# A two-layer encoder step without the products of constants in TensorE's waits

## What is computed

```python
def trunk_layer(x, pos, p, hist):
    mix, state = token_mixers(rmsnorm(x, p["g_mix_norm"]), pos, p, hist)
    x = x + mix
    return x + hier_moe(rmsnorm(x, p["g_ffn_norm"]), p), state
```

## Time and profile before

| | us |
|---|---|
| median of 3 runs (lowest to highest) | 1468.4 (1466.06 to 1472.69) |
| the profiled execution's own time | 1468.3 |
| its span, first to last instruction | 1466.5 |
| TensorE busy with matmuls | 1375.7 (94%) |
| VectorE, ScalarE, GpSimd busy | 796.3, 637.7, 91.0 |
| mean granted TensorE clock | 0.978 of 2.4 GHz |

### The profile page before, as it was taken

The page is one execution under the profiler, slowest core; times in us unless marked ns, Lnnn a source line. Parts: engine busy times, 40 slices in busy tenths (PEclk is TensorE's granted clock), DMA queues, the critical chain, the costliest instruction groups (busy, mean ns, idle before and its releaser), DMA issues.

```text
span 1466.5 us, 20830 instructions
## 1 busy us (share of the span) xinstructions
PE 1375.7 (94%) x8354; PEld 1120.0 (76%) x8354; DVE 796.3 (54%) x1156; ACT 637.7 (43%) x931; POOL 91.0 (6%) x84
## 2 busy tenths in 40 slices
PE   5998999999999989999889999999999999899996
PEld 5994666799999756776579847569999987567763
DVE  4426535633335357887663284454333443678876
ACT  4327644522324244566442385554222332455551
POOL 0300000000000011100203000000000000111002
PEclk9999899999999999999999999999999999999998
DMA  8224300033115456998912203001233153599965
GB/s 273 73 77 135 115 1 1 1 115 113 60 61 207 176 227 263 410 411 326 289 64 73 68 8 108 1 1 43 73 114 114 58 215 144 209 362 408 420 224 197
DMA packets 95447, 228.78 MB, mean 156 GB/s; under 512 B 14395, under 2 KB 64597, under 8 KB 82389
## 3 DMA queue, kind: packets, MB, share of 16 engines
q1 hardware_dynamic: 83284, 179.93, 33.8%
q0 software_dynamic: 7424, 30.94, 5.8%
q10 hardware_dynamic: 4656, 16.78, 2.8%
HBM read 199.08 MB, written 33.79 MB: 159 GB/s over the span
## 4 chain that ended last, share of the span: by engine, by line
PE 85%; ACT 5%; DVE 5%; DMA 3%; issue 2%; SPq 0%; ACTq 0%; DVEq 0%; POOLq 0%
PE ps L848 10%; PE ps L850 10%; PE ps L849 10%; PE ps L1321 8%; PE ps L1297 4%; PE ps L1299 4%; PE ps L1298 4%; PE ps L874 3%; PE ps L877 2%; PE ps L880 2%; PE ps L1142 2%; DMA rows_back<-xrow_d,row_of 2%; PE ps L1284 2%; PE ps L1199 2%; PE ps L1200 2%
## 5 line engine op out<-in xcount | busy, mean ns | idle before, releaser
L1856 DVE TENSOR_TENSOR work<-work,ps 128x544 f32<-128x544 f32 x48 | 34.6, 721 | 208.9 <-ACT work L1678 208.9
L1678 ACT ACTIVATE work<-ps 128x544 f32<-128x544 f32 x48 | 30.0, 626 | 244.9 <-PE ps L850 244.9
L849 PE MATMUL ps<-xn_r,ksv_r 128*128 128x272 f32 x384 | 110.8, 288 | 0.0
L849 PE MATMUL ps<-xn_r,work_r 128*128 128x272 f32 x384 | 110.7, 288 | 0.0
L766 POOL DMA_INDIRECT rows_back<-xrow_d,row_of x32 | 38.2, 1194 | 1107.9 <-DVE row_of L2231 891.5
L1299 PE MATMUL ps<-ew_r,rows_tok_r 128*128 128x512 f32 x256 | 100.2, 391 | 0.0
L1856 DVE TENSOR_TENSOR ew_r<-ew,gu_hi_a_r 128x2048 fp32r<-128x2048 f32 x32 | 73.1, 2290 | 15.4 <-ACT gu_hi_a_r L1701 15.4
L849 PEld LDWEIGHTS ps<-xn_r,ksv_r 128*128 128x128 f32 x384 | 72.2, 188 | 0.0
L849 PEld LDWEIGHTS ps<-xn_r,work_r 128*128 128x128 f32 x384 | 72.2, 188 | 0.0
L1701 ACT ACTIVATE gu_hi_a_r<-ew 128x2048 fp32r<-128x2048 f32 x32 | 60.7, 1910 | 5.6 <-ACT yo_b L1746 5.6
L1321 PE MATMUL ps<-ew,acts 128*128 128x512 f32 x128 | 59.4, 608 | 1.5 <-DVE acts L2348 1.5
(11 more groups left out here) (397 smaller groups left out, 3895.5 us busy)
## 6 DMA issues: line engine op xcount, KB each, us to landing
wr<-in_w_in SPq DMA_DIRECT2D x68, 512.0 KB, 4.7
ew<-in_w_exp_gate SPq DMA_DIRECT2D x32, 1024.0 KB, 6.9
ew<-in_w_exp_up SPq DMA_DIRECT2D x32, 1024.0 KB, 10.6
ew<-in_w_exp_down SPq DMA_DIRECT2D x32, 1024.0 KB
wr<-in_w_out SPq DMA_DIRECT2D x16, 512.0 KB, 4.4
rows_d<-yo_a ACTq DMA_DIRECT2D x14, 512.0 KB
rows_d<-yo_b ACTq DMA_DIRECT2D x14, 512.0 KB
rows_d<-in_zeros POOLq DMA_DIRECT2D x10, 512.0 KB, 9.2
```

The source lines that it names most:

```text
L849: mm(out_[h], w_hi, x_lo[:, c], start=False, stop=False, skip_group_check=True)
L1856: return v_.tensor_tensor(o_, a, b, op)
```

## The change

All calls of `busy` go, with the helper, and so do the two products at line 1083 with the wait on `sv_ev` ahead of head 3. Nothing is added, and nothing else is moved.

```diff
-            def busy(b, n):
-
-                for _ in range(n):
-                    mm(bank(b), ident, con[:, 0:512], start=True, stop=True, skip_group_check=True)
...
-                    if n == 10:
-                        busy(4, 2)
                     pe.wait_ge(kq_n[0], at(kq_n, l, n + 1))
...
                 pe.wait_ge(kq_ev[0], at(kq_ev, l, 12))
-                busy(6, 2)
                 suffix_high(0)
-                busy(6, 1)
                 suffix_low(0)
                 for h in range(1, SBH):
-                    if h >= 2:
-                        if h == 3:
-                            pe.wait_ge(sv_ev[0], at(sv_ev, l, 2))
-                        for _ in range(2):
-                            mm(bank(7, 448, P, 64), ident, con[:, 0:448], start=True, stop=True, skip_group_check=True)
                     suffix_high(h)
...
                 pe.wait_ge(x_mid[0], at(x_mid, l, 3))
-                busy(7, 1)
                 logits(NTILE - 2)
                 turn_mid(NTILE - 1)
                 logits(NTILE - 1)
-                busy(7, 4)
...
                 pe.wait_ge(x_mid[0], at(x_mid, l, NTILE))
-                busy(6, 1)
                 row_numbers(0, 7, 0)
-                busy(6, 1)
                 row_numbers(1, 7, 2)
-                busy(6, 5)
                 turn_rows(0, 0)
-                busy(6, 2)
                 for e in range(NE):
```

## The result

The changed kernel takes 1495.92 us (median of 4 runs, 1491.58 to 1503.55), the kernel before beside it 1467.23 (1460.77 to 1472.69). The ratio is 1.0206 with a 95% interval of 1.016 to 1.0252: **slower by 23 to 37 us**. The forecast was 1473.7, the range ended at 1482, and the largest rival stood at 1480.6. All are too low.

The account below looks back on a forecast made before the run. TensorE was taken to bound the kernel, holding 85% of the last-ending chain. Costs of 12.6 us (1.3 + 3.8 + 0.6 + 6.9) less gains of 7.15 gave +5.4 on 1468.3: 1473.7 us, range 1465 to 1482.

Parts of the forecast that it names:

- the largest rival: Stick-breaking attention stays at half clock, with twice the additional half clock (34 us, not 17): 1480.6 us, chance 0.27.
- The likeliest case: Whole kernel: clock costs of 12.6 us outweigh gains of 7.15, net +5.4 us, 1473.7 us; chance 0.45.
- the amount of half clock in the attention: Both stick-breaking attention stretches: 17.2 us more at half clock, within bounds of 0 and 96, costing 6.9 us.
- for each layer what layer 0 has now and one stay more: Attention: each layer gets 13.9 + 3.3 = 17.2 us of half clock, 34.4 in both, 17.2 more than before.
- the low end: Attention: additional half clock of 17.2 us taken nearer 0 than 96, as 28 suffix products fill TensorE for 3.56 us.
- The price of a microsecond at half clock: Attention: each microsecond at half clock loses 0.47 us where TensorE is on the chain, 85% of the span.
- the 4.9 us of gains forecast for that stage: Attention: earlier suffix sums win 2.2 us (head 0, layer 0), 1.6 (head 3, layer 0) and 1.1 (layer 1).
- the attention goes cold for good: Rival, attention: half-clock work leaves no busy stretch to restore the clock; 6.9 us more, 1480.6 us, chance 0.27.
- The gains: Attention and router to first expert: dropped products on the chain let successors start sooner, 7.15 us in all.
- The router part: Router to first expert: cold transposes 1.3, half clock from gate_up(0) 3.8, logits(3) 0.6; gains 0.6 and 1.65.
- What the profile was to show: Signs: attention clock about 0.85, router stretches 0.5 to 0.6, transposes 1.95 us, first gate_up products slow for some 4 us.
- over 22 us of additional half clock: Attention stretches: additional half clock under 5 or over 22 us would show the prediction wrong.

## Why the prediction was wrong

- *Direction*: right. The likeliest case was a loss, though I called it within 0.5%.
- *The step that failed* is the amount of half clock in the attention: "for each layer what layer 0 has now and one stay more", 17.2 us in addition. It was 83.1 - 17.2 = 65.9 us. The reason that I gave for the low end, that suffix and value products "bring the clock back", holds only with a delay that I left out: in the kernel after the stay that ends in layer 1 lasts 48 us, with 10.39 us of suffix sums in one piece and 45.5 busy us in 47.8. I took "busy" in a row for work that counts. The trace of before has both kinds of stay. Two of some 3.4 us (192.4 to 195.7, and 902.3 to 905.7) end during suffix sums with no product of constants in front, and I took one such stay more for the cost. The third, in layer 0, says otherwise (us, busy PE, PEld, DVE, ACT, POOL, clock):

```profile
161.60:171.80 10.20, 10.20 (x29) 6.66 (x29) 5.17 (x4) 8.49 (x10) 0.00 (x0) 0.50 0.56 178
```

  TensorE was busy for all of its 10.20 us at half clock. The clock came back there behind products of constants on full rows; without them, or with 64 rows in their place, this stay lasted 30.7 us (161.8 to 192.5). The prediction put that return down to the suffix sums and so took it as safe when those products go.
- *The price of a microsecond at half clock*, 0.47 x 0.85 = 0.40, was near: (21.3 + 4.9) / 65.9 = 0.40 if the 4.9 us of gains forecast for that stage came in full, and 21.3 / 65.9 = 0.32 if none did. The run without head 0's products, with a span 14.8 us longer for 58.6 - 17.2 = 41.4 us, gives 0.36. The rule of the Trainium skill that I weighed (TensorE: Matmul & The Clock Gate, HAM oscillation), half of the throttled time, would make 33 us of it; the measurement decides for the lower value.
- *The rival "the attention goes cold for good"* had the right stage and the right direction, and I gave it 0.27. Its size was wrong, 34 us of additional half clock and not 66, and so was its reason: it says that no busy stretch is left to bring the clock back, but the trace has busy stretches (45.5 of 47.8 us), and they did not do it for tens of microseconds. Nor was it for good: the clock returned in both layers before the stage ended. With 65.9 us the prediction's sum gives 65.9 x 0.40 = 26.4 and a time of 1493.
- *The gains* of 7.15 us as starts that move up: the ones I can see are there (`gate_up(0)` 0.14 us behind the split), but the kernel without head 3's products alone shows that such a gain can be lost: +0.3 to +6.5 us in place of -1.95.
- *The router part* was forecast at 1.3 + 3.8 + 0.6 - 0.6 - 1.65 = +3.5 us and cost 4 to 9. The half clock on `gate_up(0)` lasted 3.2 us in layer 0, against the forecast's 4; missed were the router products of layer 0, slower too (3.03 against 2.52), and a later stay in layer 0: `down(0)` takes 4.22 us and expert 2's transposes 1.97, against 3.44 and 1.09.
- *What the profile was to show*: the clock after the gather and the transposes (1.98) came as written; "over 22 us of additional half clock" in the attention was the mark for wrong, and it came.

## What to carry to other kernels

Products that nobody reads can be worth far more than they cost: here 51.7 us of them, of which by the prediction's count only some 7 held anything up, save about 30. Judge such filling by the clock of the stretch and not by the chain alone. In this kernel each place in the attention that was opened by itself or with one other cost time, so the longest wait alone is not enough. Look in the trace for how long the work behind a wait needed to get the clock back by itself, and whether it did so with or without the filling. More filling than the kernel had gave nothing here.

## What was unexpected of the hardware

- TensorE busy for 45.5 of 47.8 us stayed at half clock throughout. The Trainium skill says that activity releases the throttle (TensorE: Matmul & The Clock Gate, Part 1: The HAM clock gate); by these rows, time that the profile calls busy is not by itself such activity. What these suffix sums lack, which use all 128 rows, no run here shows.
- The clock can fall with next to no wait ahead. In the kernel before TensorE is busy without a gap from 156.09 on, with tile 10's transposes and then scores on 64 rows, and the clock falls at 161.6.
- Products of the same number and nearly the same length on 64 rows in place of 128 left 74 us at half clock in the two stretches, against 17, and cost 19 us. At head 0 of layer 0 they brought the clock back no sooner than no products did (192.5), where the full rows had it back at 171.8.
- One open wait of 2.28 us in each layer (tile 10) cost 11 us in all, more than twice the length of the two, by the scores and sums behind it.
